# Two chained transformer blocks on one core: the order of transfers and TensorE's work in the opening

## The reference, cut to what matters

```python
mod_x = (silu(c) @ w_mod + b_mod)[:, None, :]      # 1 x 6144: six parts of 1024
mod_c = silu(c_ctx) @ w_mod + b_mod
sh1, sc1, gt1, sh2, sc2, gt2 = split(mod_x, 6)
h_x = rmsnorm(x, g_pre_mix) * (1 + sc1) + sh1
h_c = rmsnorm(ctx, g_pre_mix) * (1 + csc1) + csh1
u_x, q_x, k_x, v_x = split(h_x @ w_in, 4)          # 256 x 512 each
u_c, q_c, k_c, v_c = split(h_c @ w_in, 4)
```

## Time and profile before

| what | value |
|---|---|
| runs | 831.69 us median of 3 (830.84 to 832.52) |
| profiled execution | span 830.1 us, first to last instruction; no other time of it is given |
| TensorE (PE) busy | 810.8 us, 98% of the span |
| DVE busy | 556.2 us, 67% |
| ScalarE (ACT) busy | 467.8 us, 56% |
| moved by the transfers | 166.27 MB, mean 200 GB/s |

### The profile page before, as it was taken

One profiled execution on the slowest core, in us unless ns is written; L12 is line 12 of the kernel. 1 busy time (PEld: TensorE's weight loads), 2 busy tenths in 40 slices (PEclk: granted clock), 3 DMA queues, 4 the chain that ended last, 5 costly groups with the idle time before them and its releaser, 6 DMA issues.

```text
span 830.1 us, 12122 instructions
## 1 busy us (share of the span) xinstructions
PE 810.8 (98%) x4442; PEld 666.1 (80%) x4442; DVE 556.2 (67%) x971; ACT 467.8 (56%) x885; POOL 44.3 (5%) x55
## 2 busy tenths in 40 slices
PE   5999999999999999999999999999999999999996
PEld 2798756788888888788888888887677888888885
DVE  2379665778877767677666665587676676676652
ACT  4582576566346553665555554675776565555542
POOL 1010000100000000100000000059000000000000
PEclk9999999999999999999999999999999999999999
DMA  9997872239887665068666554195123386666501
GB/s 353 404 384 269 359 280 72 107 116 356 288 261 236 213 199 179 28 222 268 206 196 222 190 179 164 39 354 162 46 83 128 125 279 205 206 199 207 173 1 51
DMA packets 45242, 166.27 MB, mean 200 GB/s; under 512 B 4992, under 2 KB 5120, under 8 KB 44928
## 3 DMA queue, kind: packets, MB, share of 16 engines
q1 hardware_dynamic: 44896, 164.98, 57.6%
q10 hardware_dynamic: 288, 0.52, 0.2%
HBM read 164.43 MB, written 1.05 MB: 199 GB/s over the span
## 4 chain that ended last, share of the span: by engine, by line
PE 76%; ACT 1%; issue 1%; DVE 1%; POOL 0%; POOLq 0%; ACTq 0%; DVEq 0%
PE ps L1491 24%; PE ps L1493 13%; PE ps L1518 12%; PE ps L1520 11%; PE ps L1522 11%; PE ps L1716 1%; PE ps L1760 1%; PE ps L1799 1%; PE ps L1741 1%; PE ps L1965 0%; ACT PT L528 0%; PE ps L1718 0%; PE ps L1511 0%; PE ps L1513 0%; PE ps L1512 0%
## 5 line engine op out<-in xcount | busy, mean ns | idle before, releaser
L969 DVE TENSOR_TENSOR lo<-raw,hi 128x1024 fp32r<-128x1024 f32 (+2 forms) x247 | 293.9, 1217 | 98.2 <-ACT hi L516 98.0
L1491 PE MATMUL ps<-T,hi 128*128 128x512 f32 x864 | 303.7, 392 | 0.0
L516 ACT ACTIVATE hi<-raw 128x1024 fp32r<-128x1024 f32 (+2 forms) x247 | 249.5, 1044 | 16.3 <-DMA raw<-in_w_in_v 6.9
L1493 PE MATMUL ps<-T,lo 128*128 128x256 f32 x864 | 243.5, 282 | 0.0
L1491 PEld LDWEIGHTS ps<-T,hi 128*128 128x128 f32 x864 | 162.1, 188 | 35.2
L1518 PE MATMUL ps<-hi,T 128*128 128x512 f32 (+2 forms) x500 | 169.0, 396 | 0.4 <-DVE T L1207 0.4
L1520 PE MATMUL ps<-lo,T 128*128 128x512 f32 (+2 forms) x500 | 165.6, 389 | 0.0
L1522 PE MATMUL ps<-hi,T 128*128 128x512 f32 (+2 forms) x500 | 165.4, 389 | 0.0
L1493 PEld LDWEIGHTS ps<-T,lo 128*128 128x128 f32 x864 | 163.1, 189 | 2.4
L1522 PEld LDWEIGHTS ps<-hi,T 128*128 128x128 f32 x500 | 93.8, 188 | 19.7
L1520 PEld LDWEIGHTS ps<-lo,T 128*128 128x128 f32 x500 | 93.9, 188 | 19.1
(11 more groups left out here) (219 smaller groups left out, 761.1 us busy)
## 6 DMA issues: line engine op xcount, KB each, us to landing
raw<-in_ffn_down SPq DMA_DIRECT2D x44, 512.0 KB, 3.6
raw<-in_ffn_gate SPq DMA_DIRECT2D x40, 512.0 KB, 4.2
raw<-in_ffn_up SPq DMA_DIRECT2D x40, 512.0 KB, 4.1
raw<-in_w_mlp_out SPq DMA_DIRECT2D x32, 512.0 KB, 4.4
raw<-in_w_mlp_in SPq DMA_DIRECT2D x28, 512.0 KB, 4.2
raw<-in_w_mod_p SPq DMA_DIRECT2D x24, 512.0 KB, 6.6
raw<-in_w_mod_c SPq DMA_DIRECT2D x16, 512.0 KB, 6.0
raw<-in_w_out SPq DMA_DIRECT2D x16, 512.0 KB, 4.7
```

Source lines behind the costliest of these rows:

```text
L516: e.activation(HI[SLOT[h]][:, 0:w], raw[n % RAW][:, 0:w], ACT.Copy).then_inc(s_hi, 1)
L969: e.tensor_tensor(LO[SLOT[h]][:, 0:w], raw[n % RAW][:, 0:w], HI[SLOT[h]][:, 0:w], ALU.subtract).then_inc(s_lo, 1)
L1491: e.matmul(o, a[:, k * P:(k + 1) * P], X[:, k].rearrange("p s w -> p (s w)"), start=(k == 0), stop=(k == KT - 1), skip_group_check=True)
L1493: m = e.matmul(o[:, 0:L], b[:, k * P:(k + 1) * P], Xh[:, k, :], start=False, stop=(k == KT - 1), skip_group_check=True)
```

## The change

Three things are changed. In the list of transfers the order of the opening goes from

u0, c0 to c3, u1, c4 to c7, u2, c8 to c11, u3, c12 to c15, with x ahead of all and ctx behind c15, to

c0, c1, x, c2, c3, u0, c4, c5, u1, c6 to c9, u2, c10 to c15, u3, q0, ctx, q1.

On ScalarE and DVE the splits of u1 and u2 move behind the steps on x of quarters 0 and 1, and that of u3 moves from quarter 2 to quarter 3, between the quarter's step and the step on x. In TensorE's list the products stand in pairs where they stood alone, and the blocks of one quarter closer together.

```diff
-    s = []
-    for j in range(4):
-        s += u[j:j + 1] + c[4 * j:4 * j + 4]
+    s = c[0:4] + u[0:1] + c[4:6] + u[1:2] + c[6:10] + u[2:3] + c[10:16] + u[3:4]
...
-                if n == 0:
+                if n == 2:
                     e.dma_start(x[:, :, :], t["x"].rearrange("(i p) d -> p i d", p=P)).then_inc(s_x, 16)
-                if n == CH_AT["w_in_q", 0]:
+                if n == CH_AT["w_in_q", 1]:
                     e.dma_start(cx, t["ctx"].rearrange("(i p) d -> p i d", p=P)).then_inc(s_cx, 16)
...
             for j in range(4):
                 quarter_part(j)
-                if j < 3:
+                if j == 3:
+                    split(3)
+                first_turned(0, j)
+                if j < 2:
                     split(j + 1)
-                first_turned(0, j)
...
             for j in range(4):
                 quarter_columns(j)
-                if j < 3:
+                if j == 3:
+                    split(3)
+                first_low(0, j)
+                if j < 2:
                     split(j + 1)
-                first_low(0, j)
...
             turn_rows(0, 0)
             quarter_turned(0)
-            for n in range(4, 7):
-                mod_product(n)
+            mod_product(4)
+            mod_product(5)
             turn_rows(0, 1)
+            mod_product(6)
+            u_blocks(0, 0, 2)
             mod_product(7)
-            u_blocks(0, 0, 2)
+            u_blocks(1, 0, 2)
             quarter_turned(1)
             mod_product(8)
-            u_blocks(1, 0, 1)
             mod_product(9)
-            u_blocks(1, 1, 2)
+            turn_rows(0, 2)
             mod_product(10)
-            turn_rows(0, 2)
             u_blocks(0, 2, 4)
             u_blocks(1, 2, 4)
             mod_product(11)
...
             mod_product(14)
+            mod_product(15)
             u_blocks(0, 4, 6)
-            mod_product(15)
             u_blocks(1, 4, 6)
             quarter_turned(3)
             u_blocks(2, 4, 6)
```

## The result

The changed kernel takes 832.28 us (median of 20 runs, 831.44 to 833.48), the kernel before 831.28 (20 runs, 830.43 to 832.52). The ratio is 1.0014, with a 95% interval of 1.0008 to 1.0020: slower by 1.0 us between the medians, and by 0.7 to 1.7 by the interval. The ratio is under the 0.2% that I had set as the bound of "the same". The forecast was 832.3, from 0.6 us on top of a median of 831.69; against the better median of 831.28 the same working would have said 831.9.

What follows compares the result with a forecast made beforehand. After the opening, TensorE's queue was taken to bound the kernel. Terms -0.1 - 0.25 + 1.1 = +0.75, taken as +0.6 after a possible give-back, on a median of 831.69 gave 832.3 us, own range 831.5 to 833.4.

Steps and rivals of the forecast that it cites:

- u3's wait: TensorE waits about 1.1 us for u3's low part before u3's first block; the surest term.
- Part 1: Opening transfers, c0 and c1 ahead of x, u0 behind c3: -0.1 us, bounds -0.3 and +1.2.
- Part 2: TensorE's new order from product 4 to quarter 3's turned rows: -0.25 us, bounds -0.7 and +0.3.
- the pair of products 14 and 15: In TensorE's list, running product 15 right behind product 14 saves 0.35 us.
- the wait for column 2: TensorE waits 0.45 us for modulated x before u0's block 2; with the products' saving, +0.1 us together.
- Part 3: u3's rounding behind quarter 3's columns makes u3's blocks wait: +1.1 us, bounds +1.0 and +1.2.
- Part 4: ctx one chunk later and SP's queue with its ring of seven: 0 us, bounds 0 and +0.3.
- the give-back: q1's rounding, behind the ctx scaling and not moved with TensorE, may give back up to 0.15 us.
- one of the prediction's own signs: The prediction is wrong if TensorE's durations halve elsewhere than at 21 to 23 us.
- Rival 1: TensorE's clock rises earlier, at about 18 us or before, giving 830.4 or 829.7 us; chance 0.15.
- Rival 2: u0 lands one to two chunks late and delays quarter 0: +1.3 to +2.6, middle 834.2 us; chance 0.20.
- Rival 3: The order helps and u3 isn't waited for, Part 3 near 0.2, time 831.4 us; chance 0.15.

Runs made afterwards that it cites:

- e5: The changed kernel with x's transfer ahead of all chunks again; 831.91 us, ratio 1.0009 to the kernel before.
- e6: e1 with x ahead of all and, on ScalarE, quarter 0's copy ahead of u0's rounding; 830.62 us, ratio 0.9994.
- e4: The kernel before with only TensorE's list of the changed kernel; 831.88 us, ratio 1.0004.
- e1: The changed kernel with u3's rounding behind quarter 2's step on x, on ScalarE and DVE; 831.78 us, ratio 1.0008 to the kernel before.
- e11: e1 once more, beside the changed kernel on the same chip; 831.36 us, ratio 1.0005, where the changed kernel had 832.39.
- e10: The changed kernel again, unaltered, run beside e11; 832.39 us, ratio 1.0015 to the kernel before.
- e2: The kernel before with only u3's rounding moved late, to quarter 3, on both engines; 833.25 us (5 runs), ratio 1.0033.
- e7: The kernel before with extra unread constant matmuls, 50 ahead of product 0 and 4 behind each of products 0 to 2; 832.38 us, ratio 1.0023.
- e3: The changed kernel with TensorE's list of the kernel before; 833.64 us, ratio 1.0026 to the kernel before.
- e9: The kernel before once more, unaltered, compared with itself; 831.07 us, ratio 1.0000.

## Why the prediction was right

The time was hit (832.28 for 832.3) partly by luck. The working gave +0.6 and the runs +1.0, which is 0.4 too little; the median of three from which it started was 0.4 too high. The mechanism, u3's wait as the one large term, was right.

**Part 1** (-0.1): right. Measured from the landing of the chunks, quarter 0's turned rows were 1.92 behind c3's product before and 3.06 now, and c3 comes 1.30 earlier (1.47 in the traces, less the 0.17 by which the transfers started sooner): -0.16. The reasons were the ones named: L553 at 14.18 behind u0's rounding, and the scaled x just beside it (TensorE waited for x until 14.11). Chunk c0 came at 4.64 and not at 5.8, which nobody uses. With x ahead alone (e5) 0.2 was gained. Without it the transposes couldn't start before 14.11, wherever the copy stood, and with both out of the way (e6) quarter 0 moved.

**Part 2** (-0.25, its parts bounded by -0.7 and +0.3) was the mis-sized term: it measured about +0.3, its upper end. "2 to 3", the pair of products 14 and 15, was right: -0.33 for -0.35. "1 to 2" was +0.1 in the working and measured +0.35: the wait for column 2 was 0.57 for 0.45, the products and transposes in front of it took 2.22 for 2.15, and quarter 1's turned rows took 0.97 from start to next start where they had taken 0.88. "0 to 1" was put at 0. It measured 7.90 - 7.42 - 0.71 = -0.23, but the clock rose 5.7 behind quarter 0 in place of 6.8, which at half rate is worth 0.55 (an estimate, from 1.1 us at the lower level); so +0.3. A part of it can be named: product 6 now stands alone (1.02 from 19.56 on), where three in a row took 2.72. e4 has nearly the same sizes (+0.35 and +0.26) without the rest of the change.

**Part 3** (+1.1): right, the surest term as said. "3 to ctx" +1.07, shown by taking it out (e1, e11: -1.15). The low part was ready 1.8 us behind the end of the turned rows (36.30 to 38.10), where the working had 1.75 and a little.

**Part 4** (0) and the give-back (0.15): TensorE waits for neither ctx nor the ring in the opening. From the ctx transposes to q1's first block it is 0.79 in place of 1.06: -0.27.

Sum: -0.16 + 0.3 + 0.35 - 0.33 + 1.07 - 0.27 = +0.96, against +1.0 between the medians. This sum sets the clock's rise at the same distance from quarter 0 in both. The two spans differ by 0.2 only, since in the profiled execution of before the clock rose 1.1 us later behind quarter 0 (0.55) and its transfers started 0.17 later.

By one of the prediction's own signs it failed: the durations were to halve at 21 to 23 us, and they halved at 20.7 (20.9 in e10). The forecast had counted on no change of the clock. **Rival 1** (the clock rises earlier, at about 18) did not come about, and the 1.2 to 1.5 us that it did come sooner are not shown to be due to the two early products: with the same early products it rose at 23.1 in e11 and 20.4 in e1, and with the old transfers at 14.2 in e2. (Its price had c6 and c7 at 18.8 and 20.1; the prediction's own count makes it 18.6 and 19.9.) The Trainium skill states that waits for transfers between bursts bring the lower level back (TensorE: Matmul & The Clock Gate, Part 1); e6 and e7 agree, after 1.33 and 2.28 us of waiting. **Rival 2** did not happen: u0 landed at 13.2. **Rival 3** fell with the wait at 38.10. One thing no rival had: that the wait for u3 can pull the clock down with it. It did in e2's profile; in the two profiles of the changed kernel it did not, and whether it is in its slower executions (up to 833.48) stays open.

## What to carry to other kernels

A transfer that is moved forward is worth what its first reader was waiting for, and on an engine that works in order that reader stands behind everything listed ahead of it: look for the landing that the queue waits for, not for the chunk that the product needs. A preparation that is moved behind a hand-over must be shorter than the work that covers it; here 1.75 us against 0.71 could be read from the old trace. Two parts of a change may not add: the late rounding cost at least twice as much in one order of TensorE's list as in the other. And to compare two traces by tenths of a microsecond, cut them at the same events: stretches repeated within 0.04 us where the runs of one kernel spread over 2.

## What the runs showed of the hardware

- The granted clock fell behind a wait of TensorE of only 0.84 us (e2), with turned rows of 128x2 ahead of it; behind the same wait it didn't in the changed kernel (two profiles) nor in e3 and e5.
- The clock's rise differs from execution to execution by more than the change moved it: with the same work of TensorE up to then the durations halved at 22.2 and 22.1 (before, e9) and at 14.2 (e2).
- After a fall the clock stayed low for twelve us of unbroken work (e7, 20 to 32), and extra matmuls in the first 9 us made two kernels slower (ratios 1.0023 and 1.0022).
- The profile's granted clock reads 1.00 ahead of the first rise, while a product takes 1.08 there and 0.64 after it: only the durations tell the level of the opening.
